# The last four token tiles of y as two pairs of seven products instead of whole tiles

## What is computed

```
merged = jax.nn.sigmoid(g_m) * branch_m + jax.nn.sigmoid(g_a) * branch_a
y = merged @ w_out.astype(x.dtype)
return x + rmsnorm(y, post_w)
```

## Time and profile before

| what | value |
|---|---|
| median of 3 runs | 1371.56 us (1370.78 to 1371.8) |
| profiled execution, its own time | 1369.94 us |
| its span in the trace | 1368.1 us |
| PE busy | 1352.3 us (99%), 6470 matmuls |
| PEld / DVE / ACT / POOL busy | 82% / 58% / 47% / 42% |
| granted TensorE clock, mean | 0.998 |
| start of the first matmul of y, of the last | 1274.49 us, 1362.06 us |

### The profile page before, as it was taken

One profiled execution on the slowest core, in us unless ns is written; L12 is line 12 of the kernel. 1 busy time (PEld: TensorE's weight loads), 2 busy tenths in 40 slices (PEclk: granted clock), 3 DMA queues, 4 the chain that ended last, 5 costly groups with the idle time before them and its releaser, 6 DMA issues.

```text
span 1368.1 us, 18779 instructions
## 1 busy us (share of the span) xinstructions
PE 1352.3 (99%) x6470; PEld 1127.3 (82%) x6470; DVE 794.5 (58%) x1260; ACT 641.7 (47%) x1320; POOL 569.2 (42%) x400
## 2 busy tenths in 40 slices
PE   7999999999999999999999999999999999999998
PEld 5788888888888888888888888888888888888786
DVE  5874438346543835877756575755644442997632
ACT  6644543543444455345445445544544553533421
POOL 5253435335443534654434445344333544454000
PEclk9999999999999999999999999999999999999999
DMA  6132233324233323455442634345343354966421
GB/s 194 51 76 65 69 74 90 96 48 126 76 85 72 84 79 61 149 173 144 114 145 66 188 104 134 100 127 175 87 150 97 93 188 165 345 200 196 183 97 58
DMA packets 210462, 165.02 MB, mean 121 GB/s; under 512 B 32400, under 2 KB 186544, under 8 KB 210368
## 3 DMA queue, kind: packets, MB, share of 16 engines
q1 hardware_dynamic: 210224, 163.75, 40.5%
q10 hardware_dynamic: 144, 0.07, 0.0%
HBM read 117.41 MB, written 40.08 MB: 115 GB/s over the span
## 4 chain that ended last, share of the span: by engine, by line
PE 91%; DVE 4%; issue 2%; ACT 1%; DMA 1%; SPq 1%; POOL 0%; DVEq 0%; POOLq 0%; ACTq 0%
PE proj L1244 69%; PE side L1189 3%; PE proj L1189 2%; PE side L1289 2%; PE side L1268 2%; PE side L1345 2%; PE side L1354 2%; PE proj L1170 2%; PE side L1170 2%; PE side L1277 1%; PE side L1317 1%; PE side L1350 1%; PE side L1300 1%; DMA x_sb<-x_in 1%; PE side L1362 1%
## 5 line engine op out<-in xcount | busy, mean ns | idle before, releaser
L1080 POOL TENSOR_TENSOR w_lo<-raw,w_hi 128x512 fp32r<-128x512 f32 x161 | 234.5, 1458 | 413.8 <-ACT w_hi L1456 413.7
L1244 PE MATMUL proj<-hi_T,w_hi 128*128 128x512 f32 x832 | 338.1, 406 | 2.2 <-ACT snap L1474 1.6
L1244 PE MATMUL proj<-hi_T,w_lo 128*128 128x512 f32 x832 | 325.2, 391 | 0.0
L1244 PE MATMUL proj<-lo_T,w_hi 128*128 128x512 f32 x832 | 324.1, 390 | 0.0
L1244 PE MATMUL proj<-hi_B,w_hi 128*128 128x512 f32 x624 | 254.1, 407 | 5.6 <-ACT b_sb L1518 4.0
L1244 PE MATMUL proj<-hi_B,w_lo 128*128 128x512 f32 x624 | 244.2, 391 | 0.0
L1244 PE MATMUL proj<-lo_B,w_hi 128*128 128x512 f32 x624 | 243.6, 390 | 0.0
L1080 POOL TENSOR_TENSOR w_lo<-s_sb,w_hi 128x512 fp32r<-128x512 f32 x104 | 156.7, 1510 | 153.5 <-ACT w_hi L1456 153.4
L1244 PEld LDWEIGHTS proj<-hi_T,w_hi 128*128 128x128 f32 x832 | 156.4, 188 | 36.0 <-issue 3.5
L1244 PEld LDWEIGHTS proj<-hi_T,w_lo 128*128 128x128 f32 x832 | 156.1, 188 | 34.2
L1244 PEld LDWEIGHTS proj<-lo_T,w_hi 128*128 128x128 f32 x832 | 156.6, 188 | 30.4
(11 more groups left out here) (253 smaller groups left out, 2014.5 us busy)
## 6 DMA issues: line engine op xcount, KB each, us to landing
raw<-w_in SPq DMA_DIRECT2D x95, 512.0 KB, 6.0
m_spill<-stage SPq DMA_DIRECT2D x16, 1024.0 KB, 5.6
chunk<-m_spill SPq DMA_DIRECT2D x32, 512.0 KB, 3.8
gate_spill<-stage SPq DMA_DIRECT2D x8, 1024.0 KB, 4.3
gst<-gate_spill SPq DMA_DIRECT2D x32, 256.0 KB, 3.2
share<-share_spill SPq DMA_DIRECT2D x12, 512.0 KB, 5.0
x_sb<-x_in SPq DMA_DIRECT2D x8, 512.0 KB, 7.6
hm_spill<-stage SPq DMA_DIRECT2D x4, 1024.0 KB, 8.8
```

The costliest lines, as they stand in the source:

```text
L1080: TT(w_lo_ring[k % RING][:], src, w_hi_ring[k % RING][:].bitcast(F32), ALU.subtract).then_inc(lo_pool, 1)
L1244: mm = pe.matmul(acc(p, which), w[:, kt, :], m[:, kt, :], start=(first and kt == 0 and w is wh and m is h_hi[b]), stop=(kt == 3 and w is w ...
```

## The change

Tiles 0 to 3 of y are made as before, with two slots for the split `merged` instead of four, and two PSUM slots (tensor side) instead of four. Tiles 4 to 7 become two pairs of kind "y", (4, 5) and (6, 7), appended to `seq` as 14 products (k from NK on) that run behind `output_tile(3)` with the code of the other pairs. Here the stationary blocks are the halves of `merged` rows for the two token tiles, and the moving blocks are blocks of w_out: B11, B21, B22 are read out of out_hi and out_lo, while T1 to T4, differences of 512 x 512 blocks, are new. SP loads six blocks of w_out for them again (`block_in`, 1 MB each), DVE makes the four differences (`block_sums`), ACT their high parts (`block_high`), DVE two and POOL two of the low parts (`block_low_part`), all placed under tiles 0 to 3. The first pair's S1, S2, S3 and the first four high and low parts of its products are placed directly behind the last `merged` split, ahead of everything for tile 0's result. The scale of 0.5 that `merged` carries is applied to y's tiles 4 to 7 afterwards. The pairs' tiles come out in column halves (tile 5 first, then 4; 7, then 6), are squared out of SBUF (`pair_squares`) and finished by `pair_result`. x comes back into the columns of `merged` that are no longer needed, so its first two loads now wait for mg_lo 2 and 4. Several semaphores are merged under one name each (row_sq, mean_sq, root), with offsets. The core of the diff:

```diff
+    NY = NM + (NT - YD) // 2
+    pairs += [Pair("y", i, Tile("y", 0, YD + 2 * i), Tile("y", 0, YD + 2 * i + 1)) for i in range(NY - NM)]
+    seq += plan_products(NM, NY - NM)
...
+    for b, at in (("T1", no[last, "P7"] + 1), ("T2", NK), ("T3", NK), ("T4", NK + 1)):
+        sp_late[at].append(("block_in", b))
...
                    for i, b in enumerate(FREED)]
-        merged_at = (A_W, A_W + 8192, A_W + 20480, A_W + 28672)
+        merged_at = (A_W, A_W + 8192)
...
+            if pairs[p].kind != "y":
+                return h_hi[b][:, kt, :], h_lo[b][:, kt, :]
+            if b in t_hi:
+                return t_hi[b][:, kt, :], t_lo[b][:, kt, :]
+            row, columns = (kt if b == "B11" else 4 + kt), half_of(b == "B22")
+            return out_hi[row // 2][:, row % 2, columns], out_lo[row // 2][:, row % 2, columns]
...
+                elif what == "block_in":
+                    b = it[1]
+                    w = {(k, c): w_out[k * HALF:(k + 1) * HALF, half_of(c)].rearrange("(k p) s -> p k s", p=P)
+                         for k in range(2) for c in range(2)}
...
+                        sp.wait_ge(mg_done, 16)
+                    else:
+                        sp.wait_ge(pe_prod, no[NM - 1, {"T1": "P7", "T3": "P4", "T2": "P3"}[b]] + 1)
+                    first, less = {"T1": (w[0, 1], w[0, 0]), "T3": (w[0, 1], w[1, 1]), "T2": (w[1, 1], None),
...
+                    if less is not None:
+                        sp.dma_start(t_less[b][:], less).then_inc(block_in[b], 16)
                 elif what == "post_in":
                     sp.wait_ge(pe_prod, no[KT - 1, WHOLE] + 1)
...
-                        TT(mrs[:], msq[:, h % 2], halfneg[:], ALU.pow).then_inc(m_rs, 1)
-            for t in range(NT):
-                g.wait_ge(y_ms, t + 1)
-                TT(yrs[:, t:t + 1], ysum[:, t:t + 1], halfneg[:, 0:1], ALU.pow).then_inc(y_rs, 1)
+                        g.wait_ge(mean_sq, MS_M + h + 1)
+                        TT(mrs[:], msq[:, h % 2], halfneg[:], ALU.pow).then_inc(root, 1)
+            def y_root(i):
+                t = i if i < YD else i + 1 - 2 * ((i - YD) % 2)
+                g.wait_ge(mean_sq, MS_Y + i + 1)
+                TT(yrs[:, t:t + 1], ysum[:, t:t + 1], halfneg[:, 0:1], ALU.pow).then_inc(root, 1)
+            def block_low_part(b):
+                g.wait_ge(block_hi, ("T1", "T2", "T3", "T4").index(b) + 1)
+                if b == "T1":
+                    g.wait_ge(block_sum, 2)
+                TT(t_lo[b][:], t_sum[b][:], t_hi[b][:].bitcast(F32), ALU.subtract).then_inc(block_low, 1)
+            def y_parts(p):
+                add(p, "S1")
+                add(p, "S2")
+            y_parts(NM)
+            for k in range(NK, NK + LEAD + 1):
+                if not low_dve[k]:
+                    low(k)
+            y_root(0)
+            block_low_part("T1")
+            y_root(1)
+            block_low_part("T3")
+            for i in range(2, YD):
+                y_root(i)
+            for k in range(NK, len(seq)):
+                if NK + LEAD < k + LEAD < len(seq) and not low_dve[k + LEAD]:
+                    low(k + LEAD)
+                p, name = seq[k]
+                if name == "P5" and p < NY - 1:
+                    y_parts(p + 1)
+                if name in ("P4", "P3") and p < NY - 1:
...
                     pe.wait_ge(pa_done, KT)
-                elif t == 2:
-                    pe.wait_ge(c21_done, NM)
...
-                    pe.wait_ge(c12_done, NM)
-                elif t >= 4:
-                    pe.wait_ge(y_read, 2 * t - 6)
-                hi_part, lo_part = merged_hi[t % 4], merged_lo[t % 4]
+                elif t >= 2:
+                    pe.wait_ge(y_read, 2 * t - 2)
...
                 output_tile(t)
+            for k in range(NK, len(seq)):
+                product(k)
...
+                p, name = seq[k]
+                j, half, done = {"P2": (0, 0, c11_done), "P7": (1, 1, c22_done), "P4": (1, 0, c21_done),
+                                 "P3": (0, 1, c12_done)}[name]
+                t = pairs[p].tiles[j].part
+                act.wait_ge(done, p + 1)
+                squares[0] += 1
+                act.wait_ge(row_sq, SQ_Y + squares[0] - 1)
+                A(y_junk[:], y_sb[t][:, half_of(half)], ACT.Square, scale=0.5 * DM ** -0.5,
+                  accum_out=ysq[:, t, half:half + 1]).then_inc(row_sq, 1)
+            squares = [2 * YD]
+            def block_high(b):
+                act.wait_ge(block_sum, ("T1", "T2", "T3", "T4").index(b) + 1)
+                A(t_hi[b][:], t_sum[b][:], ACT.Copy).then_inc(block_hi, 1)
             def square(t):
                 act.wait_ge(x_in[t], 16)
                 if t:
-                    act.wait_ge(x_sq, t)
-                A(tmp[0][:], x_sb[:, t, :], ACT.Square, scale=DM ** -0.5, accum_out=ssq[:, t:t + 1]).then_inc(x_sq, 1)
+                    act.wait_ge(row_sq, t)
...
                     piece(it)
             for part in range(2):
                 merged_high(1, part)
-            for t in range(NT):
-                if t + 2 < NT:
+            for k in range(NK, NK + LEAD + 1):
+                high(k)
+            HIGHS = (("T1",), ("T2",), ("T3", "T4"), ())
+            for t in range(YD):
+                y_squares(t, 0)
+                y_squares(t, 1)
+                if t + 2 < YD:
                     merged_high(t + 2, 0)
-                for half in range(2):
-                    y_squares(t, half)
+                for b in HIGHS[t]:
+                    block_high(b)
+            for k in range(NK, len(seq)):
+                p, name = seq[k]
+                after(k)
+                if k + LEAD > NK + LEAD and k + LEAD < len(seq):
+                    high(k + LEAD)
+                if name in ("P2", "P7", "P4", "P3"):
+                    pair_squares(k)
...
+                rows_ = y_sb[t][:].rearrange("p (k c) -> p k c", c=P)[:, part, :]
+                STT(rows_, rows_, yrs[:, t:t + 1], x_slot(t)[:, part, :], ALU.mult, ALU.add).then_inc(y_done, 1)
+            def pair_result(p, j, at_):
+                t = pairs[p].tiles[j].part
+                last = at_ == NT - 1
+                first, second = (0, 3) if j == 0 else (1, 2)
+                dve.wait_ge(row_sq, SQ_Y + 2 * YD + 4 * (p - NM) + second + 1)
+                STT(ysum[:, t:t + 1], ysq[:, t, 0:1], EPS, ysq[:, t, 1:2], ALU.add, ALU.add).then_inc(mean_sq, 1)
+                columns = half_of(1) if j == 0 else slice(0, DM)
+                step(STT(y_sb[t][:, columns], y_sb[t][:, columns], 0.5, pw_sb[:, columns], ALU.mult, ALU.mult))
+                dve.wait_ge(root, ROOT_Y + at_ + 1)
+                dve.wait_ge(x_in[t], 32)
+                for part in (slice(0, 4), slice(4, 8)) if last else (slice(0, KT),):
+                    with_x(t, part)
+            def block_sums(b):
+                dve.wait_ge(block_in[b], 32 if b in t_less else 16)
+                if b in ("T2", "T4"):
+                    dve.wait_ge(block_sum, 1 if b == "T2" else 2)
+                if b == "T4":
+                    ins = TT(t_sum[b][:], t_sum[b][:], t_sum["T2"][:], ALU.subtract)
+                elif b == "T2":
+                    ins = TT(t_sum[b][:], t_sum[b][:], t_sum["T1"][:], ALU.subtract)
+                else:
+                    ins = TT(t_sum[b][:], t_sum[b][:], t_less[b][:], ALU.subtract)
+                ins.then_inc(block_sum, 1)
+            def block_low_part(b):
+                dve.wait_ge(block_hi, ("T1", "T2", "T3", "T4").index(b) + 1)
+                TT(t_lo[b][:], t_sum[b][:], t_hi[b][:].bitcast(F32), ALU.subtract).then_inc(block_lo, 1)
             for part in range(2):
                 merged_low(1, part)
-            for t in range(NT):
-                if t + 2 < NT:
-                    merged_low(t + 2, 0)
-                result(t)
+            add(NM, "S3")
+            result(0)
+            merged_low(2, 0)
+            block_sums("T1")
+            block_sums("T2")
+            result(1)
+            merged_low(3, 0)
+            block_sums("T3")
+            block_sums("T4")
+            block_low_part("T2")
+            result(2)
+            block_low_part("T4")
+            result(3)
+            for k in range(NK, len(seq)):
+                if NK + LEAD < k + LEAD < len(seq) and low_dve[k + LEAD]:
+                    low(k + LEAD)
+                p, name = seq[k]
+                after(k)
+                if name == "P6":
+                    add(p, "S4")
+                if name == "P7" and p < NY - 1:
+                    add(p + 1, "S3")
+                if name == "P4":
+                    pair_result(p, 1, YD + 2 * (p - NM))
+                    dve.wait_ge(row_sq, SQ_Y + 2 * YD + 4 * (p - NM) + 1)
+                    early = y_sb[pairs[p].tiles[0].part][:, half_of(0)]
+                    STT(early, early, 0.5, pw_sb[:, half_of(0)], ALU.mult, ALU.mult)
+                elif name == "P3":
+                    pair_result(p, 0, YD + 2 * (p - NM) + 1)
```

183 lines of the change are left out of this document (108 added, 75 removed).

## The result

The changed kernel takes **1379.38 us** (median of 4 runs, 1378.8 to 1380.44), the kernel before 1371.17 us beside it (4 runs): a ratio of 1.0064, 95% interval 1.0052 to 1.0076, so slower by more than the 0.2% that can be told. The forecast was 1377.0. In proportion to the 1371.56 us shown for before, 1.0064 is 1380.3 us: the sign is the forecast one and each forecast loss shows at its place, but the sum was about 3 us short (two of its terms were too small), and the time lies at the upper edge of the range, just past it.

What follows compares the result with a forecast made beforehand. PE was taken to bound the kernel, with 91% of the chain of waits. -5.4 + 4.4 + 0.9 + 1.3 + 3.7 + 0.6 = +5.5 us gave 1375.4 us profiled, 1377.0 median; range 1371.0 to 1379.8.

Steps and rivals of the forecast that it cites:

- 24 matmuls: Tiles 4 to 7 of y: 192 matmuls become 168, saving 5.4 us on PE if PE is never late.
- POOL's turns at tile 0: Tile 0 of y: four POOL operations alternate with DVE's out_lo passes, delaying merged_lo by 4 x 1.10 = 4.4 us.
- stall behind the last P7: End of the y pairs: the last pair's P4 starts late behind P7 once more, costing 0.9 us.
- wait at the second pair's P7: Second y pair: DVE's queue readies P7 after 9.35 us, PE wants it at 8.0; +1.3 us, ends 0.4 and 2.8.
- the end: Behind the last P4: addition of x starts 5.35 us after the last matmul's end, against 1.64; +3.7 us, ends 1.5 and 4.5.
- the clock: Behind PE's wait in tile 0: granted clock falls to 0.50, costing 0.6 us, between 0 and 2.
- Rival 2: No contention at tile 0, queue in the pairs as forecast: +0.5 us, 1372.1; chance 0.12.
- rival 1: Contention only at tile 0, pair stage runs without POOL in DVE's way: +2.2 us, 1373.8; chance 0.15.
- Rival 3: Faster: DVE passes four out_lo in one go, pairs' queue drains under P3: -3.5 us, 1368.1; chance 0.05.
- Rival 4: Worse: low clock for longer, and T blocks late for P6 or P7: +9 us, 1380.5; chance 0.08.
- DVE's queue in the pairs: From first pair's P4 to second's P7: c12 starts 5.2 us after P4's end, P7 is late; +1.3 us.
- (b): Differences, high and low parts under tiles 0 to 3, costed at nothing; narrow spot: merged_lo of tile 3 slips up to 5 us.

Runs made afterwards that it cites:

- e5: Changed kernel with DVE making c12 ahead of the other tile's addition of x in the first y pair alone; 1375.51 us, 1.0038 of the kernel before.
- e2: Changed kernel with DVE making c12 ahead of the other tile's addition of x in both y pairs; 1375.61 us, 1.0031 of the kernel before.
- e6: Changed kernel with DVE making c12 ahead of the other tile's addition of x in the last y pair alone; 1379.44 us, 1.0052 of the kernel before.
- e1: Changed kernel with POOL waiting for mg_lo 2 before S1, holding back its six operations; 1374.63 us, 1.0022 of the kernel before.
- b1: Kernel before, plus six unused POOL additions of 128x512 reading SBUF behind mg_done 16; 1376.83 us, 1.0044 of the kernel before.
- e3: Changed kernel with both POOL's six operations held back and c12 first in both pairs; 1369.95 us, 0.9989 of the kernel before; run again, 1369.45 us, 0.9978.

## Why the prediction was short

Its own terms, one by one:

| term | predicted | measured | by |
|---|---|---|---|
| 24 matmuls | -5.4 | -5.4 | 6446 matmuls instead of 6470 |
| POOL's turns at tile 0 | +4.4 | +4.0 | PE's waits 4.5 against 0.5; three turns in out_lo, one ahead of merged_lo |
| stall behind the last P7 | +0.9 | +0.9 | L1578, 0.8 us, three times instead of two |
| wait at the second pair's P7 | **+1.3** | **+2.7** | L1575 (3.0 by matmul starts); e5 takes it away |
| the end | +3.7 | +3.4 | 5.05 against 1.64; e2 and e6 give back 1.9 of it |
| the clock | **+0.6** | **+1.5** | eight steps in 3.39 us |

- **Right: contention at tile 0.** Four turns of 1.10 us, read from rows of another stage, came out as three of 1.09 and one more. That the turns are taken by POOL operations which read SBUF, e1, b1 and b2 show from both sides. The rule of the Trainium skill ("SBUF — State Buffer", section on SBUF's two separate sides) taken whole, 5.2 us as an estimate, would have been too much; the turn measured around 1187 us was the better number. Rival 2 (no contention) is excluded by 7.89 us for out_lo, rival 1 (contention only there) by the rows of the pairs, where POOL's low parts hold ysum for 0.75 us and the addition of x for 2.24. Rival 3 fell with c12's 2.31 us behind the last matmul. Rival 4 had the price nearest to what came, 1380.5, and half its mechanism: the clock was low for longer. The other half, T blocks late for P6 or P7, did not come: no wait for them stands among PE's. So its price was right in part by luck.
- **Wrong: the step "DVE's queue in the pairs".** It priced the queue with each DVE operation at its undisturbed length and POOL at one power. (Its PE side has a slip of the pen as well: three products of 2.72 us are 8.15, not 8.0, so its own rows gave 1.2.) Its own upper end, "2.8, if POOL's low parts of the products get a turn here too", is what happened: the trace shows the low parts at 1346.03 and 1348.85, which lengthen ysum by 0.6 and the addition of x by 0.96 us, and a high part on ACT puts the square off by 0.4 us. c12 starts 6.9 us behind the start of ACT's copy c21 (1344.83), where the step had 5.2 behind P4's end. The rows for this were there: the same scheme makes low parts on POOL three products ahead all through the kernel.
- **Wrong: the size of the step "The clock".** It laid a good part of the low stretch into the wait. The fall came in the last us of the wait, so nearly the whole low stretch lay on matmuls: 1.5 us instead of 0.6. The size is no constant of this wait either: e2 and b1, with the same 4.18 us, lost 2.2 us.
- **Costed at nothing, and not nothing once tile 0 is repaired: the "narrow spot" of (b).** The step left some 4 us before PE would want merged_lo of tile 3. In the changed kernel PE did not wait for it, but tile 0's long wait had put PE back by nearly 6 us; with that gone (e1, e3) it waited 0.2 us, and 1.2 in the second run of e3.
- **Partly missed: a scatter of 1 us** at the start of the program in the profiled execution, which no forecast of one execution could hold; from out_lo on the change costs 7.8 us, and the sum with the two terms put right is -5.4 + 4.4 + 0.9 + 2.7 + 3.7 + 1.5 = 7.8. The ratio's interval, 1.0052 to 1.0076, is 7.1 to 10.4 us, so the 7.8 lie in it. The medians say 1 us more than this. The mean granted clock of the single executions points at the low clock: of the changed kernel's nine executions the two at 0.991 are the slowest beside their own (1380.44 and 1382.42 us), and of e6's six the three at 0.992 and 0.993 took 1380.2 to 1380.6 us, the three at 0.995 and 0.996 only 1376.1 to 1378.7. Where they had it no trace shows, so this is likely and not shown.

## What to carry to other kernels

Work put on an idle GpSimd is not free when it reads SBUF beside VectorE passes with two SBUF inputs: each of its operations costs such a pass one turn (here 1.1 us), so look for the stretch where VectorE sets TensorE's pace and start the GpSimd work behind it; one wait did that here, worth 5.9 us by the timed runs and some 4 by the one profile. Afterwards look again at what that wait had hidden: here the tile 3 wait came up. When a scheme with fewer matmuls moves sums of results to another engine, put the sum that the next product or the end waits for at the head of that engine's queue, ahead of finished tiles' last steps; here the same operations in another order were worth 4.7 us. Only with both was the saving of matmuls seen in the time. And before a difference of a few us between two profiles is given to a cause, look up where the granted clock fell in each.
